# A residual stream turned onto token partitions, output projections into four held PSUM banks, and a filter moved into a feed-forward

## What is computed

```python
for l in range(2):
    g = norm_gains[l]
    h = rms_norm(x, g[0])
    mix = even_mixer(h) if l == 0 else fox_attention(h)      # both end in "@ w_out"
    x = x + rms_norm(mix, g[1])
    h = rms_norm(x, g[2])
    x = x + rms_norm(conv_ffn(h, ...), g[3])                 # 1024 -> 2 x 2816 -> 1024
```

```python
h = rms_norm_2(x, g_pre) * (1 + scale) + shift
y = mixer(h) @ w_out
x = x + gate * rms_norm_2(y, g_post)
```

## Time and profile before

| | us |
|---|---|
| three runs | 1870.31, 1870.34, 1871.42 |
| median | 1870.34 |
| the profiled execution | 1871.38 |
| its span, first to last instruction | 1869.7 |
| PE busy | 1694.0 (91%) |
| DVE busy | 1187.7 (64%) |
| ACT busy | 875.0 (47%) |
| POOL busy | 205.9 (11%) |
| DMA, mean rate | 115 GB/s |
| mean granted clock of PE | 0.952 of 2.4 GHz |

### The profile page before, as it was taken

One profiled execution on the slowest core, in us unless ns is written; L12 is line 12 of the kernel. 1 busy time (PEld: TensorE's weight loads), 2 busy tenths in 40 slices (PEclk: granted clock), 3 DMA queues, 4 the chain that ended last, 5 costly groups with the idle time before them and its releaser, 6 DMA issues.

```text
span 1869.7 us, 25639 instructions
## 1 busy us (share of the span) xinstructions
PE 1694.0 (91%) x10176; PEld 1452.4 (78%) x10176; DVE 1187.7 (64%) x1969; ACT 875.0 (47%) x1497; POOL 205.9 (11%) x240
## 2 busy tenths in 40 slices
PE   6986899979997999969999988899995899999997
PEld 6874899958886999926867766688883778988886
DVE  5656788457656887375565766634647656657774
ACT  5664566444444665443312544333325254556653
POOL 0001111011101111030000000000012021113211
PEclk9987899989998999979999989999998999999998
DMA  6522565644226555523310212232330223332242
GB/s 213 182 68 102 184 184 185 183 167 147 79 91 204 170 180 182 159 88 113 101 35 23 80 67 90 79 90 90 102 99 20 84 68 102 93 104 91 86 135 91
DMA packets 61559, 215.71 MB, mean 115 GB/s; under 512 B 6528, under 2 KB 9856, under 8 KB 61312
## 3 DMA queue, kind: packets, MB, share of 16 engines
q1 hardware_dynamic: 61440, 214.07, 35.6%
HBM read 213.00 MB, written 1.05 MB: 114 GB/s over the span
## 4 chain that ended last, share of the span: by engine, by line
PE 62%; issue 16%; DVE 11%; ACT 6%; POOL 4%; DMA 0%; POOLq 0%; DVEq 0%; SPq 0%; ACTq 0%
PE PS L313 17%; PE PS L315 17%; PE PS L314 17%; PE PS L1602 1%; PE PS L1611 1%; DVE TMP L445 1%; PE PS L396 1%; POOL AR L2287 1%; ACT L368 1%; DVE WL L289 1%; DVE AR L557 1%; POOL AR L2290 1%; POOL AR L2292 1%; ACT WH L278 1%; PE PS L1224 1%
## 5 line engine op out<-in xcount | busy, mean ns | idle before, releaser
L313 PE MATMUL PS<-RH,WH 128*128 128x256 f32 (+1 forms) x2528 | 802.3, 317 | 78.9 <-DVE WL L289 42.7
L314 PE MATMUL PS<-RH,WH 128*128 128x256 f32 (+1 forms) x2528 | 791.1, 313 | 0.0
L315 PE MATMUL PS<-RH,WL 128*128 128x256 f32 (+1 forms) x2528 | 790.5, 313 | 0.0
L289 DVE TENSOR_TENSOR WL<-RAWB,WH 128x1024 fp32r<-128x1024 f32 x346 | 430.3, 1249 | 255.3 <-ACT WH L278 250.0
L313 PEld LDWEIGHTS PS<-RH,WH 128*128 128x128 f32 x2528 | 493.6, 195 | 118.3 <-ACT WH L278 43.6
L314 PEld LDWEIGHTS PS<-RH,WH 128*128 128x128 f32 x2528 | 494.0, 195 | 24.3 <-issue 0.5
L315 PEld LDWEIGHTS PS<-RH,WL 128*128 128x128 f32 x2528 | 493.0, 195 | 25.0
L278 ACT CAST WH<-RAWB 128x1024 fp32r<-128x1024 f32 x346 | 358.0, 1039 | 162.7 <-PE PS L315 122.2
L571 POOL TENSOR_TENSOR TMP<-TMP 128x256 f32<-128x256 f32 (+1 forms) x36 | 31.0, 862 | 788.1 <-ACT TMP L531 788.0
L1134 DVE SCALAR_TENSOR_TENSOR AR<-PS,PR,AR 128x255 f32<-128x255 f32 (+1 forms) x176 | 84.8, 482 | 38.4 <-ACT AR L1089 35.3
L1089 ACT ACTIVATE AR<-PS,PR 128x256 f32<-128x256 f32 x88 | 49.8, 566 | 101.4 <-PE PS L315 98.2
(11 more groups left out here) (317 smaller groups left out, 2006.4 us busy)
## 6 DMA issues: line engine op xcount, KB each, us to landing
RAWB<-ws SPq DMA_DIRECT2D x394, 512.0 KB, 3.6
CS<-cs SPq DMA_DIRECT2D x1, 1472.0 KB, 8.4
X<-xT SPq DMA_DIRECT2D x1, 1024.0 KB, 5.8
X<-ctxT SPq DMA_DIRECT2D x1, 1024.0 KB, 8.3
AR<-dec SPq DMA_DIRECT2D x2, 512.0 KB, 7.7
outT<-X SPq DMA_DIRECT2D x2, 512.0 KB, 2.9
AR<-rgw SPq DMA_DIRECT2D x1, 512.0 KB, 5.5
AR<-fw SPq DMA_DIRECT2D x2, 256.0 KB, 6.9
```

The source lines that it names most:

```text
L289: dve.e.tensor_tensor(k.WL[:, i % SPL, :], k.RAWB[:, i % RAW, :], k.WH[:, i % SPL, :].bitcast(F32), ALU.subtract).then_inc(*dve.done("wl", i))
L313: pe.e.matmul(o, wh, xh, start=first, stop=False)
L314: pe.e.matmul(o, wh, xl, start=False, stop=False)
L315: return pe.e.matmul(o, wl, xh, start=False, stop=last)
```

## The change

`X` becomes 4 blocks of 128 tokens by 1024 channels. A norm's statistics are then columns: ACT squares 512 channels with a running sum (`squares_act`), and roots are one element per partition. `outnorm_*` and `prenorm_*` are gone. In their place:

- `out_pe`: four PSUM banks (2 token blocks x 2 halves of the channels) are held (`Ring.hold`) and every contraction block is added to them as soon as its operand is there, with the operand stationary and 512 columns of weights moving. The last three contraction blocks run bank by bank, but in a feed-forward one block at a time.
- `seam_act`, `seam_dve`, `seam_pe`: norm, residual, second norm, scaling of token rows, transposes to channel partitions, gain and split. The gains that were columns on partitions become rows, loaded by ACT's DMA queue (`gains_act`) or made by TensorE from columns (`gate_rows_pe`).
- In a feed-forward the down-projection of block j - 3 follows the up-projections of block j, so no separate down phase is left.
- Modulation: 48 units of 128 columns, one chunk each, 8 contraction blocks. Units 0 to 15 stand in `ffn0` (j = 1 to 16), 16 to 31 in the first projections of `even2`, 32 to 47 in its last ones. None is left in the attention.
- The filter's 16 steps stand in `ffn1` at j = 5 to 20, the context's norm at j = 12, its transposes and splits at j = 13 to 16. Its weights and decay are loaded by ACT's queue, in two halves.
- `even2` projects both halves of its output with tokens on partitions (4 banks of 128 tokens each, twice); `last_tokens_pe` finishes one bank after the other.

```diff
@@ project out
-def outnorm_pe(k, pe, s, name, kt, k0, rhs, ready, N, tail=None):
-    for m in range(8):
-        project(k, pe, (s, "out", m), name, kt, m, rhs, N, ready, k0)
...
+def out_pe(k, pe, s, name, ks, kt, lhs, ready):
+    if ks[0] == 0:
+        for tb in range(2):
+            for h in range(2):
+                k.ps.hold(pe, s, "out", tb, h)
...
+        if i < kt - 3:
...
+            for tb in range(2):
+                for h in range(2):
+                    mm = three(pe, k.ps.of(s, "out", tb, h), lhs(i, tb), (w[0][:, half(h)], w[1][:, half(h)]), i == 0, False)
@@ the chain between two stages
+SEAM = [("squares", 0), ("root", 0), ("add", 0), ("squares", 1), ("squares2", 0), ("root", 1), ("add", 1), ("root2", 0),
+        ("scale", 0), ("squares2", 1), ("root2", 1), ("scale", 1)]
...
+def seam_act(k, act, m):
+    for what, n in m.steps():
+        tb = 2 * m.q + n
+        if m.s and m.t and (what, n) in (("add", 1), ("scale", 1)):
+            cast_to(k, act, m.opens(k) + (what == "scale"))
...
+def root_dve(k, dve, s, kind, tb):
+    dve.e.tensor_scalar(c0, w, r, r, ALU.mult, ALU.mult)
...
+    dve.e.tensor_scalar(c0, c0, -0.5, 1.5, ALU.mult, ALU.add)
...
+    dve.e.tensor_tensor(r, r, c0, ALU.mult)
+def residual_dve(k, dve, s, tb, h, src, gain):
+    dve.e.scalar_tensor_tensor(t, src, stat(k, s, "o", tb)[3], gain, ALU.mult, ALU.mult)
...
+    dve.e.tensor_tensor(x, x, t, ALU.add)
+def turn_pe(k, pe, s, q, i, n, turned, take=True):
...
+    for j in range(2):
+        t = pe.e.transpose(b[:, 256 * j + 128 * n:256 * j + 128 * n + 128], turned[:, c:c + 128], k.ident)
@@ modulation
 def mod_pe(k, pe, u):
-    l, c = divmod(u, 6)
+    l, c = divmod(u, 24)
...
     for i in range(8):
-        w, end = weights(k, pe, False, f"w_mod{l}", i, 4 * c, 4)
+        w, end = weights(k, pe, False, f"w_mod{l}", i, c)
         g = 32 * (i % 4)
-        mm = pe.e.matmul(b[g:g + 32, :], k.SCC[:, 2 * i:2 * i + 32], w, start=i < 4, stop=i > 3)
+        mm = pe.e.matmul(b[g:g + 32, 0:128], k.SCC[:, 2 * i:2 * i + 32], w, start=i < 4, stop=i > 3)
@@ ffn_pe
     for j in range(22):
         for m in (j, j + 22):
             project(k, pe, (s, "up", m), f"ffn_up{l}", 8, m, operand(L.HH), 256, ready)
-        if j == 0:
-            mod_turn_pe(k, pe, L.unit)
+        if ffn_mod(l, j) is not None:
+            mod_pe(k, pe, ffn_mod(l, j))
+        if ffn_mod(l, j - 1) is not None:
+            mod_turn_pe(k, pe, ffn_mod(l, j - 1))
...
+        if ffn_filter(l, j) is not None:
+            filter_pe(k, pe, *FILTER_STEPS[ffn_filter(l, j)])
...
+        if j >= FFN_LAG:
+            down(j - FFN_LAG)
@@ ffn_act
+            if ffn_filter(l, j) is not None:
+                filter_act(k, act, *FILTER_STEPS[ffn_filter(l, j)])
+            if ffn_ctx(l, j) == -1:
+                ctx_act(k, act)
...
+            if j >= FFN_LAG:
+                out_ahead(k, act, s, [j - FFN_LAG], cast_to)
@@ even2, odd2 norms (DVE)
+    for tb in range(4):
+        mix(tb, 1)
+        mean_dve(k, dve, s, "o", tb)
+        root_dve(k, dve, s, "o", tb)
+        for h in range(2):
+            residual_dve(k, dve, s, tb, h, L.MIX[:, tb, half(h)], L.GP[tb // 2][:, half(h)])
+        mean_dve(k, dve, m.t, "p", tb)
+        root_dve(k, dve, m.t, "p", tb)
+        for j in range(8 if tb % 2 else 0):
+            whole_dve(k, dve, m.t, m.q, j, m.gain(j), m.shift(j))
+            if m.q == 0 and j % 3 != 2:
+                low_of_whole(k, dve, m.t, m.q, j, m.high(j), m.low(j))
```

More of the change, by code:

```diff
@@ L110, in take, with hold, drop @@
         return self.tiles[i]
+    def hold(self, eng, *name):
+        tile = self.take(eng, *name)
+        self.held.add(self.place[name])
+        return tile
+    def drop(self, *name):
+        self.held.discard(self.place[name])
     def of(self, *name):
@@ L359, in blocks, with stat, half, squares_act @@
     return lambda i, n: tuple(v[:, i, n * 128:n * 128 + 128] for v in hl)
+STAGES = ["even", "ffn0", "fox", "ffn1", "even2", "odd2"]
+def stat(k, s, kind, tb):
+    a = 5 * (((STAGES.index(s) % 2) * 2 + "op".index(kind)) * 4 + tb)
+    return [k.NS[:, a + i:a + i + 1] for i in range(5)]
+def half(h):
+    return slice(512 * h, 512 * h + 512)
+def squares_act(k, act, s, kind, tb, h, src):
+    junk = k.junk.take(act, s, kind, tb, h)
+    act.e.activation(junk, src, ACT.Square, accum_out=stat(k, s, kind, tb)[h]).then_inc(*act.done(s, kind, tb, "ss", h))
+    k.junk.free(act, s, kind, tb, h)
@@ new lines, with __init__, opens, steps @@
+class Seam:
+    def __init__(self, s, t, gain, shift=None, turned=None, hh=None, q=0):
+        self.s, self.t, self.gain, self.shift, self.turned, self.hh, self.q = s, t, gain, shift, turned, hh, q
+    def opens(self, k):
+        return k.ws.opens(self.t, *{"even": ("f", 0), "fox": ("fc",), "even2": ("x1", 0), "odd2": ("gate", 0)}.get(
+            self.t, ("up", 0)))
+    def steps(self):
+        return [x for x in SEAM if (self.s or x[0] in ("squares2", "root2", "scale")) and
+                (self.t or x[0] in ("squares", "root", "add"))]
+    def high(self, j):
+        return self.hh[0][:, j, 256 * self.q:256 * self.q + 256]
+    def low(self, j):
+        return self.hh[1][:, j, 256 * self.q:256 * self.q + 256]
@@ new lines, in seam_dve @@
+def seam_dve(k, dve, m, gain=0, rows=None):
+    for what, n in m.steps():
+        tb = 2 * m.q + n
+        if what == "root":
+            mean_dve(k, dve, m.s, "o", tb)
+            root_dve(k, dve, m.s, "o", tb)
+        elif what == "add":
+            dve.wait_ge(k.s_gain, 32 * gain)
+            for h in range(2):
+                residual_dve(k, dve, m.s, tb, h, k.ps.of(m.s, "out", tb, h),
+                             rows[h] if rows else k.T[4 + h][:, :])
+                k.ps.free(dve, m.s, "out", tb, h)
+        elif what == "root2":
+            mean_dve(k, dve, m.t, "p", tb)
+            root_dve(k, dve, m.t, "p", tb)
+        if m.s and m.t and (what, n) in (("add", 1), ("scale", 1)):
+            rest_to(k, dve, m.opens(k) + (what == "scale"))
+    if m.t and not m.shift:
+        for j in range(8):
+            low_dve(k, dve, m.t, m.q, j, m.high(j), m.low(j), m.gain(j))
@@ L422, in prenorm_high_act @@
[L422 to L435, removed]
@@ L438, in prenorm_scale_dve @@
[L438 to L458, removed]
@@ L991, in even_dve @@
     dve.mark(s, "mixed")
-    for j in range(4):
-        ahead("half", j)
+    out_ahead(k, dve, s, range(4), rest_to)
     for j in range(4):
@@ L1167, in ffn_pool @@
             L.GV.free(pool, s, j + 22)
-    outnorm_pool(k, pool, s, L.MIX, 256)
-    pool.mark(s, "end")
+    if l == 1:
+        m = seams(k)["even2"]
+        for j in (2, 5):
+            low_of_whole(k, pool, m.t, 0, j, m.high(j), m.low(j))
 class Fox:
```

956 lines of the change are left out of this document (538 added, 418 removed).

## The result

The changed kernel takes **1893.5 us** (median of four runs, 1892.7 to 1895.8) against 1870.9 before (1870.3 to 1873.0): ratio 1.0121, interval 1.0103 to 1.0138. It is slower by 1.2%; I had forecast 1849, faster by 1.1%, with an upper bound of 1886. Its profiled execution took 1895.8 us with a span of 1893.5.

What follows compares the result with a forecast made beforehand. The prediction took TensorE's instruction stream and its standstills to bound the kernel. Savings in seams, end and attention against costs of filter, modulation and waits summed to -21.4 us: 1849 us by the median, range 1814 to 1886.

Steps and rivals of the forecast that it cites:

- Seams, end, seam before even2: Norm chains between stages: first three seams together -21.4 us, end 15.1 to 8.8 (-6.3), seam before even2 -49.7.
- Second feed-forward: Filter and context inside it: matmuls +25.5 us, transposes +2.2, waits +8 (3 to 20), output projection -3.5; together +32.2.
- First feed-forward: 16 modulation units 14.4 us, +2 for the margin on low parts, output projection -3.5: together +12.9.
- The seam before odd2: Chain through four token blocks, DVE starting 12.3 us before the last matmul: 29.0 to 36 us, +3.2; bounds -5, +9.
- Even: Cast of the last weight chunk waits for TensorE's block 4; last operand at 160 us instead of 156, +2.7 net.
- the term of the units: 48 modulation units of 128 columns inside TensorE's stream, 0.9 us each: +43.2; bounds 0.7 and 2.2 a unit.
- Rivals 1: Weight loads of the small modulation units are not hidden, 0.44 us more each, 21 in all: 1870, no change; chance 0.07.
- 2: A small modulation unit costs like the big one, 2.2 us with its turn, 62 more: 1911; chance 0.10.
- Attention: In even2, three modulation units and 11.6 us of waits for weights' low parts go: counted 29 us, taken as -24.
- The start: Norm chain entered later, two casts and two table loads ahead of ACT's squares: 20.7 to about 23 us, +2.
- Odd2: Rest of the stage: output projection -2.5 us, no stop for a late operand -2.2, gate rows +1.8; together -2.9.
- Rival 3: Feed-forwards' weight splits queue behind other ACT and DVE work, 1.0 us in each of 44 periods: 1883; chance 0.15.

Runs made afterwards that it cites:

- The leaving out: The changed kernel without even2's 32 modulation units (matmuls, turns, rows, weight chunks), the second modulation being the bias alone: 1849.3 us.

## Why the prediction was wrong

Neither of the two signs that I had named came: the longer feed-forward is 232.6 us (over 235 was the sign), and odd2's seam did not fall under 25 but rose. The misses lie in terms for which I had no sign.

**Seams, end, seam before even2: right.** The price of the chain by single operations gave 17.1, 19.1, 17.1, 19.1 and 8.8 us; measured are 16.4, 19.1, 16.4, 19.2 and 8.4.

**Second feed-forward: right in kind and size,** +35.6 for +32.2. TensorE waited 10.1 us for low parts in seven places, where I had 8 in five; that they come from the queue in front of the splits is shown by the order with the splits first, 5.7 us shorter. **First feed-forward,** +13.8 for +12.9, and its margin at the unit's bank is real: the same order cost 9 there.

**The seam before odd2: the step that failed.** It was "DVE ... starts 12.3 us before the last matmul". The chain itself was sized nearly rightly: 48.3 us by my sum (12.3 + 36), 50.4 measured from the first addition (1410.7) to the first projection (1461.1). But it started 1.4 us behind the last matmul, since I priced what the chain holds and not what stands in front of it on its queues: the opening splits of odd2, and the ring place they wait for. I had seen this very wait in even. The run with the splits moved gave 12.9 of the 15.2 us back.

**Even: the step named, the size wrong.** I wrote that the cast "holds ACT and DVE in the middle of the gate's chain" and put the last operand at 160 us; it came at 171.3 (DVE's low part), 4.3 of it from the later start. I had the wait, but took TensorE's block 4 at full clock: its 12 matmuls ran from 155.7 to the release at 160.3, 4.6 us for 12 x 0.227 = 2.7, and the cast comes behind them. That is 1.9 of the 7 us that are left; the other 5 are not taken apart. About 8 us were to be had, as the later split showed.

**Even2: the term of the units, undersized.** 48 x 0.9 = 43.2. The leaving out gives 39.8 for 32 units where I had 28.8: 0.1 us more for each, and some 7 us at the two last, which I did not look at one by one; 6.0 of these came back when their turns were moved. The 0.1 was a slip in my own sum: four rounds of 0.11 and the 0.2 to fill that I had read from the big unit make 0.64, and I wrote 0.5 to 0.55; measured are 0.65. Rivals 1 (1.34 us a unit) and 2 (2.2 us) are both out: with a quarter of the columns the 16 entries take 0.65 us for 1.92. The Trainium skill (TensorE: Matmul & The Clock Gate, What overlaps and what doesn't) says that a weight load overlaps matmuls in flight only when its row group differs. The trace does not bear that rule out here either: by my estimate exposed loads would have made 1.34.

**Attention: -24 against -21.3** (207.0 to 185.7 us). The waits for weights went as said, and "a wait for DVE may be next" came true: 7.6 us at L1819, the rotation's wait for normed keys and queries, were 4.0 at the same instruction before.

**The start: the right cause, half the size.** +4.3 for +2. Two casts and two table loads stand ahead of the squares, as I wrote; that the first of them waits until 9.5 us for its weights while the tokens lie there from 4.3 on I did not put together.

**Odd2: not wrong, as far as can be told.** With its first matmuls it was to lose 6.5 us; measured are +0.1 in the profiled pair and -5.2 between the means (424.0 twice before, 418.8 over eight after). The changed kernel's second execution, whose clock over the stage (0.98) is that of the kernel before, took 6.8 us less. So the 7.0 us that the table books as a miss here are for the most part the clock of that one execution, and say little about the forecast. What starts the longer stretches at half clock in some executions is open.

**Rival 3 was not what happened,** though its time (1883) was the nearest: the feed-forwards' weight pipeline cost 10, not 44. Its mechanism, splits in a queue behind work that is not yet due or in front of work that is, acted at five places that I had costed at nothing or little: odd2's seam, even's gates, the start, the second feed-forward's side steps, and, turned round, the first feed-forward's banks. By order alone 12.9 + 8 + 9.7 + 6.0 + 5.7 = 42 us were to be had, the two last turns among them, each measured in an edit of its own. That is not the miss split up, since the start and even had some of it before; it is what the changed kernel's queues still held.

## What to carry to other kernels

Price a chain by its operations, then write down for each engine what is queued in front of its first instruction and which event releases that. A split that runs ahead waits for a ring place at the worst moment, the end of a stage, and holds the epilogue behind it: put it behind the first block's chain. Look at the last instance of a repeated step by itself, since the cover of all the others, the next step's work, is missing there. And an order that helps one stage (splits first) costs in another that gives banks back on the same queue: try each stage alone.

## What the runs showed of the hardware

- Sixteen fp32 matmul entries of 128 columns in four column groups take 0.65 us, and with a two-column matmul of a full weight load behind them delay a dense stream by 1.0; with 512 columns they took 1.92.
- One and the same stage took 417 to 424 us in executions of the same instructions, with the length of the stretches at half clock behind its gaps differing (a mean clock of 0.73 against 0.84 over 32 us, 0.86 against 1.00 over 36), the lower of the two levels being 1.2 GHz.
- In the first 9 us DMA brings the tokens at 4.3 and the first weight chunk at 9.0 to 9.5 us; work on the tokens fits in between whole.
